# Reordering layer 0 of a two-layer Fourier / S5 / MoE block: read-out powers after the chunk scan, projection products moved, GLU on packed tokens

## The reference

```python
p = a @ w_in                                  # columns: fourier 512 | ssm 512 | gate a 1024 | gate b 1024
y_ssm = gelu(d * u + sum over 2 directions of Re(scan(u @ b_bar, lam_bar) @ c_mat))   # 32 groups, 64 states
g_a, g_b = sigmoid(p[gate a]), sigmoid(p[gate b])
y_a = fourier_mix(p[fourier]) @ w_four
y_b = (y_ssm @ w_glu_a) * sigmoid(y_ssm @ w_glu_b)
out = (g_a * y_a + g_b * y_b) @ w_out
```

## Time and profile before

| | |
|---|---|
| median of 3 runs | 2355.86 us (2350.47 to 2357.87) |
| the profiled execution, its time | 2355.88 us |
| its span, first to last instruction | 2354.1 us |
| mean granted TensorE clock | 0.964 of full |
| TensorE busy | 2208.4 us (94%) |
| VectorE busy | 1395.7 us (59%) |
| ScalarE busy | 933.9 us (40%) |
| moved by DMA | 536.49 MB, 228 GB/s |

### The profile page before, as it was taken

The page is one execution under the profiler, slowest core; times in us unless marked ns, Lnnn a source line. Parts: engine busy times, 40 slices in busy tenths (PEclk is TensorE's granted clock), DMA queues, the critical chain, the costliest instruction groups (busy, mean ns, idle before and its releaser), DMA issues.

```text
span 2354.1 us, 26149 instructions
## 1 busy us (share of the span) xinstructions
PE 2208.4 (94%) x10092; PEld 1603.3 (68%) x10092; DVE 1395.7 (59%) x1857; ACT 933.9 (40%) x839; POOL 0.2 (0%) x4
## 2 busy tenths in 40 slices
PE   4887999997999999989998899999999999999995
PEld 1444563233677778758956788888888888888884
DVE  4565716423322233327212788889888888888886
ACT  0220212101222122111000676767667666777673
POOL 0000000000000000000000000000000000000000
PEclk9898999999899999999799899999999999999998
DMA  8343644312153541337442598989999999989894
GB/s 342 58 165 122 133 155 173 125 72 107 72 197 143 197 191 68 116 71 207 125 152 99 221 374 336 367 338 360 345 362 346 340 357 351 374 321 374 331 376 156
DMA packets 84588, 536.49 MB, mean 228 GB/s; under 512 B 23040, under 2 KB 50304, under 8 KB 52992
## 3 DMA queue, kind: packets, MB, share of 16 engines
q1 hardware_dynamic: 62688, 513.89, 59.8%
q10 hardware_dynamic: 21792, 21.01, 2.6%
HBM read 516.59 MB, written 18.28 MB: 227 GB/s over the span
## 4 chain that ended last, share of the span: by engine, by line
PE 87%; DVE 5%; DMA 5%; ACT 1%; issue 1%; SPq 0%; ACTq 0%; DVEq 0%
PE ps L1471 21%; PE ps L1773 13%; PE ps L1774 13%; PE ps L1783 13%; PE ps L1480 5%; PE ps L1484 5%; PE ps L1487 5%; PE ps L1604 2%; PE ps L1705 1%; PE ps L1727 1%; PE ps L1407 1%; DMA aT<-in_pos 1%; PE ps L1719 1%; DMA cks<-CW 1%; PE ps L1589 1%
## 5 line engine op out<-in xcount | busy, mean ns | idle before, releaser
L1311 DVE TENSOR_TENSOR WL<-mring,WH 128x2048 fp32r<-128x2048 f32 x340 | 763.4, 2287 | 112.8 <-ACT WH L821 111.9
L821 ACT ACTIVATE WH<-mring 128x2048 fp32r<-128x2048 f32 x340 | 632.6, 1912 | 143.5 <-PE ps L1783 107.0
L1773 PE MATMUL ps<-WH,XGh 128*128 128x512 f32 x896 | 357.3, 399 | 6.3 <-issue 3.7
L1774 PE MATMUL ps<-WH,XGl 128*128 128x512 f32 x896 | 349.2, 390 | 0.0
L1471 PE MATMUL ps<-aT,ring 128*128 128x512 f32 (+1 forms) x768 | 271.6, 515 | 22.5 <-ACT aT L707 22.5
L1471 PEld LDWEIGHTS ps<-aT,ring 128*128 128x128 f32 x768 | 147.6, 194 | 141.2 <-issue 129.9
L1783 PE MATMUL ps<-WL,XGh 128*128 128x512 f32 x896 | 221.6, 389 | 0.0
L1773 PEld LDWEIGHTS ps<-WH,XGh 128*128 128x128 f32 x896 | 168.3, 188 | 41.8 <-issue 5.0
L1141 DVE TENSOR_TENSOR ringl<-ring,FWH 128x4096 fp32r<-128x4096 f32 (+2 forms) x19 | 73.4, 3864 | 205.6 <-ACT FWH L693 205.6
L1783 PEld LDWEIGHTS ps<-WL,XGh 128*128 128x128 f32 x896 | 168.2, 188 | 34.9
L1774 PEld LDWEIGHTS ps<-WH,XGl 128*128 128x128 f32 x896 | 168.4, 188 | 33.4
(11 more groups left out here) (241 smaller groups left out, 2238.7 us busy)
## 6 DMA issues: line engine op xcount, KB each, us to landing
mring<-in_moe_gate SPq DMA_DIRECT2D x58, 2048.0 KB, 9.6
mring<-in_moe_up SPq DMA_DIRECT2D x57, 2048.0 KB, 9.7
mring<-in_moe_down SPq DMA_DIRECT2D x56, 2048.0 KB, 9.7
ring<-in_w_mod SPq DMA_DIRECT2D x24, 2048.0 KB, 8.6
ring<-in_w_in SPq DMA_DIRECT2D x12, 2048.0 KB, 10.4
ring<-in_ffn_gu SPq DMA_DIRECT2D x11, 2048.0 KB, 10.4
cks<-CW ACTq DMA_DIRECT2D x16, 512.0 KB, 3.6
ring<-cks SPq DMA_DIRECT2D x4, 2048.0 KB, 13.0
```

Source lines behind the costliest of these rows:

```text
L821: nc.scalar.activation(WH[buf][:, o], mring[t % MRING][:, o], ACT.Copy).then_inc(high_done, 1)
L1311: V.tensor_tensor(WL[buf][:, o], mring[t % MRING][:, o], WH[buf][:, o].bitcast(F32), ALU.subtract).then_inc(low_done, 1)
L1773: mm(out_, ah, WH[buf][:, o:o + 512], start=(first and q == 0), stop=False)
L1774: mm(out_, al, WH[buf][:, o:o + 512], start=False, stop=False)
```

## The change

Nothing of the arithmetic changes but the order of sums and columns. In words:

1. VectorE runs the parameter chain first; positions and squares come behind it.
2. `out_powers(0, k)` and the lag rows move behind the chunk scan, on TensorE `lags(0, n)` from between the products of gate a to between the first four of gate b. Of gate a, the second four products move behind the L1552 block. `H[:, 0]` is cleared behind the copies.
3. The read-outs of layer 1 get two buffers, as layer 0 has; `CW1` and `LB1` lie over `BP0` and `BWs` now.
4. The GLU products read `pack` as it lies; VectorE's product with `G2` reads `aT` through the view instead.
5. The `w_mod` tiles and their sums move: tiles 8 and 9 to before Y, 10 and 11 before and after `glub`, none behind `glua`; in the FFN one tile of weights later. `pack_load` comes two ring loads later; `toep_load` comes behind the first `ck` tile.
6. `weights_low(1)` moves from behind residual 6 to behind the second norm; ACT waits for the mix before `weights_high(0)`.

```diff
         side([("turn", 0, n, r) for n in range(ITS) for r in range(2)])
-        side([("lag", 0, mh) for mh in range(2)])
         side([("E", 0, m, d) for m in range(4) for d in range(2)])
...
+        side([("lag", 0, mh) for mh in range(2)])
         side([("Y", 0, mh, c) for mh in range(2) for c in range(2)])
...
-        stream += [("toep", 0, 0), ("ck", 0, 0), ("ck", 0, 1), ("w_four", 0, 0)] + mods(8)
+        stream += [("ck", 0, 0), ("toep", 0, 0), ("ck", 0, 1), ("w_four", 0, 0)] + mods(10)
...
-            stream += [key] + (mods(FFN_MOD + i) if FFN_MOD + i < ADA_TILES else [])
+            stream += [key] + (mods(FFN_MOD + i - 1) if 0 < i <= ADA_TILES - FFN_MOD else [])
...
+        work1 = ExitStack()
+        CW1 = sb(work1, "CW1", [P, 2, 4, (CHUNK + 1) * SG])
+        LB1 = sb(work1, "LB1", [P, 4, 2, 32])
+        work1.close()
         BP0 = sb(mix, "BP0", [P, 2, 4, P])
...
                 for m in range(8):
                     evac(("gb", l, m), G2[:, m, t0:NT], ACT.Sigmoid, n)
+                    if l == 0 and m < 4:
+                        for i in range(2 * m, 2 * m + 2):
+                            store_reads(0, i)
+                        if m == 3:
+                            store_lags(0, 0)
+                        for i in range(2 * m + 2, 2 * m + 4):
+                            if i < ITS:
+                                masked(0, i)
+                    if l == 0 and m == 4:
+                        store_lags(0, 1)
+                        act.wait_ge(b_masked, 2 * ITS)
+                        act.dma_start(raw[:].rearrange("p a r c h -> p (a r c h)"), a["bc"][1]).then_inc(raw_in, 16)
...
-            dve.wait_ge(params_in, 2 * 16)
-            link(V.tensor_tensor(hT[:, :, CTX:NT], hT[:, :, CTX:NT], aT[:, :, 0:SEQ], ALU.add))
-            for m in range(KD):
-                V.tensor_tensor(aT[:, m, :], hT[:, m, :], hT[:, m, :], ALU.mult).then_inc(sq_ready, 1)
             dve.wait_ge(table_in, 2 * 16)
...
             link(V.tensor_tensor(wv[:, 1, :], z[3], d1, ALU.mult))
+            dve.wait_ge(params_in, 2 * 16)
+            link(V.tensor_tensor(hT[:, :, CTX:NT], hT[:, :, CTX:NT], aT[:, :, 0:SEQ], ALU.add))
+            for m in range(KD):
+                V.tensor_tensor(aT[:, m, :], hT[:, m, :], hT[:, m, :], ALU.mult).then_inc(sq_ready, 1)
...
                 if l == 0:
                     mod_columns(1)
+                    for k in range(ITS):
+                        out_powers(0, k)
+                        if k == 5:
+                            lag_rows(0, 0)
+                    lag_rows(0, 1)
                     tables(1)
...
-                    link(V.tensor_tensor(G2[:, m, t0:NT], G2[:, m, t0:NT], aT[:, m, t0:NT], ALU.mult))
+                    g2 = G2[:, m, t0:NT].rearrange("p (c j) -> p c j", j=CHUNK)
+                    link(V.tensor_tensor(g2, g2, aT[:, m, t0:NT].rearrange("p (j c) -> p c j", j=CHUNK)[:, :, ::-1], ALU.mult))
...
-                    if l == 0 and m in (3, 6):
-                        weights_low(m // 5)
+                    if l == 0 and m == 3:
+                        weights_low(0)
...
-                b = n % 2 if l == 0 else 0
+                b = n % 2
...
-                        product((name, l, m), [(w[:, k, P * m:P * m + P], ys_in_order[k]) for k in range(MB)], n_)
+                        product((name, l, m), [(w[:, k, P * m:P * m + P], pack[:, k, 0:CHUNK * n]) for k in range(MB)], n_)
```

More of the change, by code:

```diff
@@ L732, in _ @@
                     for k in range(4, 8):
-                        i = 2 * (k - 4)
                         evac(("ga", l, k), G[:, k, t0:NT], ACT.Sigmoid, n)
[L735 to L744, removed]
+                        if k == 5:
+                            mod_rows(6)
                 for m in range(4):
                     evac(("f", l, m), uF[:, m, t0:NT], cols=n)
-                if l == 0:
-                    store_lags(0, 1)
-                    mod_rows(7)
+                    if l == 0 and m == 1:
+                        mod_rows(7)
                 for m in range(4):
@@ L1003, in tables @@
                 if l:
-                    for r in range(2):
-                        _, done, _, at, _ = place(("turn", 0, ITS - 2, r))
-                        dve.wait_ge(done, at + 1)
+                    dve.wait_ge(cw_stored[1], 16 * 4)
                 flat = BP0[:].rearrange("p r g c -> p (r g c)")
@@ L1066, in out_powers @@
                             dve.wait_ge(y_stored[mh], 16 * CHUNK)
-                if n >= back:
-                    dve.wait_ge(lags_done, ITS * l + n - back + 1)
-                    dve.wait_ge(cw_stored[b], 16 * (n // 2 if l == 0 else 4 + n))
+                if n == 1:
+                    for r in range(2):
+                        _, done, _, at, _ = place(("turn", l, ITS - 1, r))
+                        dve.wait_ge(done, at + 1)
+                    if l == 1:
+                        dve.wait_ge(bw_stored, 16 * ITS)
+                if n >= 2:
+                    dve.wait_ge(lags_done, ITS * l + n - 1)
+                    dve.wait_ge(cw_stored[b], 16 * (4 * l + n // 2))
                 v = CWs[b][:].rearrange("p r g (k h) -> p r g k h", h=SG)
@@ L1507, in _, with gate_a @@
                         mod_sums(4)
+                def gate_a(k):
+                    w = slot(("w_in", l, 2 + k // 4))[:].rearrange("p (k c) -> p k c", k=KD)
+                    product(("ga", l, k), [(w[:, q, P * (k % 4):P * (k % 4) + P], aT[:, q, t0:NT]) for q in range(KD)], n_)
                 if l == 0:
                     mod_turn(4)
-                    for k in range(8):
-                        w = slot(("w_in", l, 2 + k // 4))[:].rearrange("p (k c) -> p k c", k=KD)
-                        product(("ga", l, k), [(w[:, q, P * (k % 4):P * (k % 4) + P], aT[:, q, :]) for q in range(KD)])
-                        for i in range(2):
-                            if k < 4:
-                                turn(0, 2 * k + i)
-                            else:
-                                lags(0, 2 * (k - 4) + i)
+                    for k in range(4):
+                        gate_a(k)
+                        turn(0, 2 * k)
+                        turn(0, 2 * k + 1)
                         if k == 1:
@@ L1615, in _ @@
                 if l == 0:
-                    mod_sums(8)
-                    mod_turn(8)
-                ys_in_order = [pack[:, k, 0:CHUNK * n].rearrange("p (j c) -> p c j", j=CHUNK)[:, :, ::-1] for k in range(MB)]
+                    mod_sums(10)
                 for name in ("glub", "glua"):
```

103 lines of the change are left out of this document (58 added, 45 removed).

## The result

| | before | after |
|---|---|---|
| median | 2354.14 us (4 runs, 2350.47 to 2357.87) | 2269.53 us (4 runs, 2267.78 to 2271.16) |
| ratio, 95% interval | | 0.964 (0.9622 to 0.9659) |
| profiled execution: time, span | 2355.88, 2354.1 us | 2270.69, 2268.9 us |
| mean granted clock | 0.964 | 0.958 |

The change is faster by 84.6 us. The forecast was 113 us faster (2242.5), and its range (2222 to 2263) was missed by 6.5 us. The table compares the two timelines of TensorE, cut where its stages begin (the prediction's terms sorted into the same stretches; 5.7 us of sums and turns pass from behind Y to ahead of it, so they shift between the second and the fourth row).

The account below looks back on a forecast made before the run. TensorE, 87% of the chain, was taken as the bound. Terms -10.2 -4.7 -15.9 +11 +3 -58.6 -27.8 +3.2 -13.3 sum to -113.3, taking 2355.9 to 2242.5 us; range 2222 to 2263.

Parts of the forecast that it names:

- Parameter chain: VectorE's chain at the start, moved ahead of the wait for xT and pos: first reciprocal from 61.2 to 51.0, -10.2 us.
- The ring's order: Ahead of the gates: w_mod tile 5 loads before pack, ending TensorE's 3.3 us wait and the slow sum, -4.7 us.
- Read-outs behind the scan: Layer 0: input-power matmuls stop waiting for lag rows, read-outs stand between gate-b products; this part sums to -15.9 us.
- The reload: Lag rows reloaded before layer 0's Y: they land at 298 to 302, so Y waits 8 to 12 us, +11.
- the signs that the prediction named for being wrong: Y starting by 291 or after 310, glub products over 5 us apart, or FFN waits for weights.
- The clock in Y: Layer 0's Y: after the reload wait the clock is halved for some us only, +3 us.
- Y stays at half clock throughout: Rival for layer 0's Y: half clock for all of it, 19 us more than forecast, 2261; chance 0.13.
- GLU of layer 0: Gate products reading pack contiguously save 57.1 us; with waits gone and 2 us lost at lag rows, -58.6.
- The prediction's third rival: Two buffers do not speed layer 1's read-outs, their stores coming late beside GLU tiles: +26, 2268; chance 0.07.
- GLU of layer 1: Layer 1's 16 gate products, 55.63 us before, read pack contiguously at 0.43 instead of 0.87 per matmul: -27.8 us.
- End of the mixer: Layer 0: last mix less hidden, +3.2 us; second low half of weights off the path before the sum of squares, -13.3.
- Nothing in the FFN: Shifted w_mod tiles in the FFN cost nothing: as many sums, each slot freed at the same point of a tile.

Follow-up runs that it names:

- the last kernel: Changed kernel with layer 0's read-outs begun earlier, w_mod tile 6 held behind the input-power block and w_glu_a behind the sixth chunk-power store: 2229.80 us, ratio 0.9461.
- The kernel without gaps: Changed kernel with the load of w_mod tile 6, and the w_in tile behind it, held back until the input-power block is through: 2263.80 us, ratio 0.9622.

## Why the prediction was right and wrong, by its steps

- **Parameter chain**, -10.2: right. The first product starts at 56.38, and alone it gave 9.5.
- **The ring's order**, -4.7: right. The sum for tile 5 waits for nothing and takes 1.90 us.
- **Read-outs behind the scan**, -15.9: the wait for the lag rows is gone. The read-outs beside gate b wait 5.2 us. The products behind the two waits take 8.83 us at a clock of 0.81 and 15.33 at 0.91, where others take 7.13 and 14.00 at 1.00: some 3 more, 8 in all where 7 was taken. What the step did not count is what runs beside the block: in its new place two 2 MB loads do (issued at 125.42 and 125.82; DMA share 0.76 from 128.3 to 140), and it has gaps of 3.4 us. Before, it restarted when the loads were over (DMA share 0.00 and 0.03 from 203 on, rows in the last section) and had none. The cover held: VectorE was free at 202 (near 199 forecast).
- **The reload**, +11: Y waits 9.24. TensorE was ready at 296 (290 forecast; the gaps and the slower read-outs are most of it), Y starts at 305, inside the forecast's 291 to 310. So the signs that the prediction named for being wrong did not see the failure of the next term: none of them asked for Y's length or clock. The reload was issued from 281.26 and Y started at 305.13: 23.9 us, near the 22 that the prediction took from its row of 107 GB/s.
- **The clock in Y, +3: this is the step that failed.** It was sized "as behind the wait of 10.9", by the block of input powers, which had recovered within 5 us of its restart. Y did not recover in 41.7 us, at 0.50 throughout. The term measured +19.7, with +2.6 in the first product behind it. The rival *Y stays at half clock throughout* had mechanism and price (19 more, 2261) with a chance of 0.13; the row that spoke for it, layer 1's part at 0.50 throughout (13.87 us), is the same instruction as Y's with half the columns, the row that spoke against it another one. The nearer row should have been taken, though it was no full match either: layer 1's Y has no wait ahead of it, and its clock falls from 1.00 to 0.50 while TensorE is busy.
- **GLU of layer 0**, -58.6: `pack` costs what `G` does, and the two buffers keep pace, with nothing lost at the lag rows (+2 taken). But "these now have two buffers" does not hold at the second read-out. The second buffer shares memory with the staging of the `bps` store: 7.25 and a product slower by 1.5. The prediction's third rival had stores of 14 us beside GLU tiles, but at every read-out, not at one. The two waits for `bw_stored` ahead of that buffer (L605, L1075) are what the change adds, and the prediction did not price them.
- The permutation costs VectorE something after all: 1050 ns for the product that reads `aT` through the view, 692 for the one without a stride, a factor of 1.5 (0.36 us a product), where TensorE's busy time had paid 2. Groups by shape of VectorE in after, 430 to 470 us:

```profile
L1239 DVE TENSOR_TENSOR GR<-GR,aT 128x512 f32<-128x512 f32 x8 | 8.4, 1050 | 0.3
L1240 DVE TENSOR_TENSOR G<-G,GR 128x512 f32<-128x512 f32 x8 | 5.5, 692 | 0.3
```

  It costs nothing here: VectorE is idle 0.9 us or more in each product.
- **GLU of layer 1**, -27.8: right, 27.79 us from 1135.55 instead of 55.63, and -27.7 from the FFN to the end.
- **End of the mixer**: the mix waits 1.88 us without any loss of clock (1.00 from 465.87 to 470), so +1.9 for +3.2. The -13.3 is right in size. Its cause was not the one named, or not it alone: with the tile loaded earlier the low half's place did nothing (2269.15 with it back), and the prediction did not see the earlier load.
- **Nothing in the FFN**: right within the scatter of 3 us.

Summed over the profiled executions, 85.2 us faster where 113.3 was forecast: 16.7 (Y) + 2.6 (product behind it) + 8.8 (store) - 2 (lag rows of layer 1) + 3.4 (gaps) + 1.3 (read-outs) - 1.8 (shorter wait at Y) - 1.3 (mix) = 27.7 of the 28.1 us that the forecast was off. The rival of Y at half clock, taken alone, gives 2261, inside the range; with the late store and the gaps on top the time fell outside.

## What to carry to other kernels

What a wait costs is read from a row of the very instruction behind it, for it was more than its own length here: 9 us of waiting ahead of Y cost 22 more, where 10.9 ahead of the block of input powers had cost under 2. A dozen matmuls for nothing, or a producer begun some products earlier, bought them back (Y 19.6 us shorter with either). A new buffer is a second buffer only once whatever else lives in its memory has left (7.25 us of waiting and 1.5 in the product behind it here); look there for the store that is on its way. And moving a big load away from a store is worth little if it lands on the next store that somebody waits for: VectorE's wait of 10.21 us became one of 0.83 and one of 8.37, and the time stayed at 2270.14.

## What the hardware showed that I had not expected

- Y of layer 0 kept the clock with which it was entered: 41.70 us, continuously busy, at 0.50 (the changed kernel; the one before with an added wait, 41.70 too), and 22.10 at 1.00 when TensorE had been busy before it (the one with the extra matmuls). Other stages came back to full clock while TensorE was busy, and Y, as busy in the records, did not. Of the blocks of 512-column products of `glub` in the changed kernel, the first one behind the wait of 7.25 took 5.21 us at 0.70, and the next one 3.70 at 1.00. The block of input powers, 64 columns too, came back to full clock behind its wait of 10.9. Y of layer 1, 32 columns a matmul, was entered at full clock behind 55.42 us of products without a wait, and lost it, down to 0.50, while TensorE was busy. The view by stretches of the kernel before shows both, the block first (the clock is the third number from the end); what tells these stages apart no run shows:

```profile
203.00:205.00 2.00, 2.00 (x44) 2.00 (x42) 0.69 (x1) 0.00 (x0) 0.00 (x0) 0.50 0.00 0
205.00:207.00 2.00, 2.00 (x66) 2.00 (x64) 1.38 (x2) 0.00 (x0) 0.00 (x0) 0.87 0.00 0
207.00:210.00 3.00, 3.00 (x104) 2.93 (x98) 2.09 (x4) 0.00 (x0) 0.00 (x0) 1.00 0.03 5
...
1139.00:1142.00 3.00, 3.00 (x29) 2.97 (x28) 0.00 (x0) 1.67 (x2) 0.00 (x0) 1.00 0.63 158
1142.00:1145.00 3.00, 3.00 (x43) 2.96 (x42) 0.00 (x0) 0.00 (x0) 0.00 (x0) 0.86 1.00 429
1145.00:1150.00 5.00, 5.00 (x50) 5.00 (x50) 0.00 (x0) 0.00 (x0) 0.00 (x0) 0.50 0.17 72
```

- A store of 512 KB came late beside big loads on another queue. The median of the chunk-power stores of the changed kernel is 3.3 us from issue to landing. The last `bps` store, issued at 391.48 behind two loads of 2 MB, held VectorE until 401.91, 10.4 us; with one load under way (issued at 387.81) the same store, issued at 391.08, held it until 397.50, 6.4 us; one issued at 419.08 just behind `w_glu_a` until 429.74, 10.7 us. The number of loads does not set it: in the last kernel a store issued at 340.17, with one load under way since 339.39, took 9.2 us. In all four the store was through 10 to 12 us after the latest load ahead of it had been issued.
- Gaps of 1 to 2 us with no releaser in a run of short matmuls went away with the 2 MB loads beside them. The instruction queue has transfers of 16 KB at 132.0 and 137.1 us, ahead of the gaps that end at 134.23 and 139.34; that TensorE waited for these is likely, and no run shows it by itself. The kernel without gaps has such transfers in its block too, beside no load.
